# First attention on keys and values brought out of the latents, two heads at once on halves of the array, with the search, the decays and the second block's latents reordered

## What is computed

```python
# dsa_attention: cq (256 wide) and ckv (128 wide) are normed latents
q = jnp.einsum('btr,rhd->bthd', cq, w_uq)                        # 8 heads of 64
q_abs = jnp.einsum('bthd,hcd->bthc', q, w_uk) * (HD_ATT ** -0.5)
_, sel = lax.top_k(score, topk)                                  # 256 of the causal keys
logits = (jnp.einsum('bthc,btkc->bthk', qa, kv_sel) + bias)      # bias: by head and distance
p = jax.nn.softmax(logits, axis=-1)
o = jnp.einsum('bthk,btkc->bthc', p, kv_sel)
return jnp.einsum('bthc,hcd->bthd', o, w_uv)
# second block: q_lat and kv_lat are 384 and 256 wide, k_rope 32
q = (_rmsnorm(q_lat, g_q_lat[i]) @ w_q_up[i]).reshape(bsz, s, N_HEADS, QK_DIM)
kv = (_rmsnorm(kv_lat, g_kv_lat[i]) @ w_kv_up[i]).reshape(bsz, s, N_HEADS, NOPE_DIM + V_DIM)
```

## Time and profile before

| | us |
|---|---|
| median of 3 runs (3828.99 to 3829.85) | 3829.42 |
| the profiled execution | 3827.32 |
| its span | 3826.0 |
| PE, DVE, ACT, POOL busy | 3473.7, 1779.5, 917.6, 345.7 |

### The profile page before, as it was taken

One profiled execution on the slowest core, in us unless ns is written; L12 is line 12 of the kernel. 1 busy time (PEld: TensorE's weight loads), 2 busy tenths in 40 slices (PEclk: granted clock), 3 DMA queues, 4 the chain that ended last, 5 costly groups with the idle time before them and its releaser, 6 DMA issues.

```text
span 3826.0 us, 51800 instructions
## 1 busy us (share of the span) xinstructions
PE 3473.7 (91%) x21830; PEld 2725.6 (71%) x21846; DVE 1779.5 (47%) x2886; ACT 917.6 (24%) x1666; POOL 345.7 (9%) x277
## 2 busy tenths in 40 slices
PE   6989658887889899999997898999999999999998
...
GB/s 202 43 67 209 127 18 52 36 41 12 17 56 61 116 55 48 47 50 83 94 132 57 34 1 23 50 28 50 37 90 132 55 50 45 50 45 115 143 105 149
DMA packets 216071, 270.22 MB, mean 71 GB/s; under 512 B 11068, under 2 KB 176226, under 8 KB 215587
## 3 DMA queue, kind: packets, MB, share of 16 engines
...
...
## 4 chain that ended last, share of the span: by engine, by line
PE 75%; DVE 8%; ACT 3%; issue 2%; POOL 0%; DMA 0%; DVEq 0%; ACTq 0%; POOLq 0%
PE psum L1934 17%; PE psum L1936 17%; PE psum L1938 17%; PE psum L2951 3%; PE psum L1174 3%; PE psum L1706 2%; PE psum L1729 2%; PE psum L2800 2%; PE psum L2448 2%; PE psum L2654 2%; PE psum L2822 2%; PE psum L2811 1%; PE psum L1717 1%; PE psum L1192 1%; PE psum L1760 0%
## 5 line engine op out<-in xcount | busy, mean ns | idle before, releaser
L1934 PE MATMUL psum<-hT_hi,wcut_lo 128*128 128x512 f32 x1856 | 588.9, 394 | 16.8 <-DVE hT_lo L1973 16.8
L1938 PE MATMUL psum<-hT_lo,wcut_hi 128*128 128x512 f32 x1856 | 582.0, 390 | 0.0
L1936 PE MATMUL psum<-hT_hi,wcut_hi 128*128 128x512 f32 x1856 | 581.9, 390 | 0.0
L1934 PEld LDWEIGHTS psum<-hT_hi,wcut_lo 128*128 128x128 f32 x1856 | 350.0, 189 | 96.7 <-DVE hT_lo L1973 17.9
L1938 PEld LDWEIGHTS psum<-hT_lo,wcut_hi 128*128 128x128 f32 x1856 | 349.8, 188 | 73.4
L1936 PEld LDWEIGHTS psum<-hT_hi,wcut_hi 128*128 128x128 f32 x1856 | 350.1, 189 | 72.7
L1916 DVE CAST wcut_hi<-raw 128x1024 fp32r<-128x1024 f32 x256 | 176.9, 691 | 475.0 <-PE psum L1938 450.5
L1934 PE MATMUL psum<-wcut_hi,xcut_lo 128*128 128x512 f32 x1120 | 348.1, 392 | 19.0 <-DVE xcut_lo L2052 13.8
L1936 PE MATMUL psum<-wcut_hi,xcut_hi 128*128 128x512 f32 x1120 | 346.7, 391 | 0.0
L1938 PE MATMUL psum<-wcut_lo,xcut_hi 128*128 128x512 f32 x1120 | 346.5, 391 | 0.0
L1033 POOL TENSOR_TENSOR st<-st,nhalf 128x1 f32<-128x1 f32 (+2 forms) x78 | 62.0, 802 | 3046.3 <-DVE st L674 3046.3
...
## 6 DMA issues: line engine op xcount, KB each, us to landing
...
```

The costliest lines, as they stand in the source:

```text
L1934: pe.matmul(outs[i], al, bs[i][0], start=start, stop=False, skip_group_check=True)
L1936: pe.matmul(outs[i], ah, bs[i][0], start=False, stop=False, skip_group_check=True)
L1938: mm = pe.matmul(outs[i], ah, bs[i][1], start=False, stop=stop, skip_group_check=True)
```

## The change

It has three parts. Lines of the changed kernel differ from those of before by up to 45.

**RWKV.** The search gets 2 steps a round up to round 20 and then 1, after the round's own work; `Pe` goes ahead of `mx`, `PC` ahead of the square of `kk`; PE no longer waits for the fence `rwkv_start`.

```diff
+    K.wuk, K.wuv = r.take("wuk", 8, 64), r.take("wuv", 8, 64)
+    r, mid, last = region(HI0 + 4224, W1), region(2 * SLOT, 4 * SLOT), region(4 * SLOT, 5 * SLOT)
+    K.qT1 = [r.take("qTa", 1024) for _ in range(2)]
+    K.kT1 = [r.take("kTa", 1024)]
...
-    K.ya = r.take("ya", 8, 512)
+    K.Va, K.kT1 = r.take("Va", 8, 512), K.kT1 + [r.take("kTa", 1024)]
...
+    K.Mh += [mid.take("Mh", 1024) for _ in range(2)]
+    K.Lg += [last.take("Lg", 1024), e.take("Lg", 1024)] + [mid.take("Lg", 1024) for _ in range(2)]
...
+
+
+def best_steps(g):
+
+    return 2 if g < 21 else 1
...
     if j == 2:
+        v.wait_ge(*S.at(("Pi", t)))
+        v.scalar_tensor_tensor(Pe, sig, 0.5 * E05, bank(K, 7), MUL, ADD).then_inc(*V.up(("Pe", t)))
         v.wait_ge(*G.at(("mixed", t)))
         v.tensor_tensor(mx, mx, K.prev[:, 0:1024], ADD).then_inc(*V.up(("mx", t)))
-        v.wait_ge(*S.at(("Pi", t)))
-        v.scalar_tensor_tensor(Pe, sig, 0.5 * E05, bank(K, 7), MUL, ADD).then_inc(*V.up(("Pe", t)))
...
         s.wait_ge(*V.at(("Pe", t)))
         s.activation(K.Pes[t % 3], K.Pes[t % 3], ACT.Exp, bias=K.mask("shift")[:, 2:3]).then_inc(*S.up(("Pe", t)))
+        s.wait_ge(*T.at(("tot", t)))
+        s.activation(K.PCs[:, t % 4, :], p[:, 0:8], ACT.Exp, bias=K.mask("shift")[:, 3:4]).then_inc(*S.up(("PC", t)))
         if t:
             s.wait_ge(*V.at(("bonus", t - 1)))
         s.wait_ge(*V.at(("kk", t)))
         s.activation(K.tmp, K.kk, ACT.Square).then_inc(*S.up(("kk", t)))
-        s.wait_ge(*T.at(("tot", t)))
-        s.activation(K.PCs[:, t % 4, :], p[:, 0:8], ACT.Exp, bias=K.mask("shift")[:, 3:4]).then_inc(*S.up(("PC", t)))
...
 def rwkv_tensor(pe, K):
-    rwkv_start(pe, K)
     pe.wait_ge(*K.D["mk"].at("mk"))
...
     for g, tiles in rounds_of():
-        if g < BEST_ROUNDS:
-            for _ in range(3):
-                next(K.best, None)
-        if g == BEST_ROUNDS:
-            for _ in K.best:
-                pass
         for t, r in tiles:
...
                 front_vector(v, K, t, r)
+        if g < BEST_ROUNDS:
+            for _ in range(best_steps(g)):
+                next(K.best, None)
+        if g == BEST_ROUNDS:
+            for _ in K.best:
+                pass
```

```diff
-ATT = [(h, t) for h in range(8) for t in range(NT)]
+ORDER = (4, 3, 5, 2, 6, 1, 7, 0)
+ATT = [(q, t) for q in range(4) for t in ORDER]
...
-        sp.wait_ge(*V.at(("max", h - 2, NT - 1)))
+        if h >= 4:
+            sp.wait_ge(*V.at(("max", 8 * (h // 2) - 9, h % 2)))
         distances_load(sp, K, h)
-    sp.wait_ge(*T.at(("qa", 7)))
-    loads_to(sp, K, "w_out", 3, "w_out")
+        if h == 5:
+            sp.wait_ge(*T.at(("query", 3, 1)))
+            loads_to(sp, K, "w_out", 3, "w_out")
+    fence(sp, K, "att")
...
+def query_tensor(pe, K, q, j, b):
+
...
+    pe.wait_ge(*B.free(b))
+    if j < 2:
+        for k in range(2):
+            mm = pe.matmul(bank(K, b), w[:, k, q * 128:(q + 1) * 128], K.cqT2[:, k, hs], start=k == 0, stop=k == 1, skip_group_check=True)
+    else:
+        mm = pe.matmul(bank(K, b), K.wuk[:, 2 * q:2 * q + 2, :].rearrange("p a b -> p (a b)"), K.ckvT2[:, hs], start=True, stop=True,
+                       skip_group_check=True)
+    mm.then_inc(*T.up(("query", q, j)))
+    B.until(b, S if j < 2 else V, ("query", q, j))
...
+def values_tensor(pe, K, t, b):
...
+    pe.wait_ge(*B.free(b))
+    pe.matmul(bank(K, b), K.ckvT2[:, t * 128:(t + 1) * 128], K.wuv.rearrange("p a b -> p (a b)"), start=True, stop=True,
+              skip_group_check=True).then_inc(*T.up(("values", t)))
+    B.until(b, S if t % 2 else V, ("values", t))
...
+def scores_tensor(pe, K, r):
...
+    for b in range(4):
+        pe.wait_ge(*B.free(b))
+    for o in range(0, W, 512):
+        n = min(512, W - o)
+        for par in range(2):
+            d = slice(64 * par, 64 * par + 64)
+            mm = pe.matmul(bank(K, 2 * par, 2)[:, o:o + n], K.qT1[q % 2][d, t * 128:(t + 1) * 128], K.kT1[q % 2][d, o:o + n], start=True,
+                           stop=t < 2, skip_group_check=True)
+            if t < 2:
+                mm.then_inc(*T.up(("qk", r, par)))
...
+        pe.wait_ge(*V.at("maskb"))
+        for par in range(2):
+            for o in range(0, W, 512):
+                n = min(512, W - o)
+                mm = pe.matmul(bank(K, 2 * par, 2)[:, o:o + n], K.idbf, K.maskb[:, MOFF[t] + o:MOFF[t] + o + n], start=False, stop=True,
...
+            mm.then_inc(*T.up(("qk", r, par)))
+    for par in range(2):
+        for b in (2 * par, 2 * par + 1):
+            B.until(b, V, ("max", r, par))
...
+def turned_tensor(pe, K, r, par):
...
+    L = K.Lg[2 * (r % 3) + par]
+    pe.wait_ge(*V.at(("norm", r, par)))
...
+        for k in range(g0, min(t + 1, g0 + 4)):
+            tr = pe.transpose(bank(K, b)[:, (k - g0) * 128:(k - g0 + 1) * 128], L[:, k * 128:(k + 1) * 128], K.ident)
...
+def outputs_tensor(pe, K, r):
...
+    pe.wait_ge(*B.free(6))
+    for par in range(2):
+        pe.wait_ge(*S.at(("pT", r, par)))
+    for b in range(t + 1):
+        for par in range(2):
+            mm = pe.matmul(bank(K, 6)[64 * par:64 * par + 64, 0:128], K.Va[:, b, (2 * q + par) * 64:(2 * q + par + 1) * 64],
+                           K.pT[2 * (r % 2) + par][:, b, :], start=b == 0, stop=b == t, skip_group_check=True)
+    mm.then_inc(*T.up(("pv", r)))
+    B.until(6, V, ("mixed in", r))
...
+    for j in range(4):
+        query_tensor(pe, K, 0, j, 7 - j)
+    for t in range(NT):
+        values_tensor(pe, K, t, t if t < 4 else 11 - t)
+    for r in range(len(ATT) + 3):
+            turned_tensor(pe, K, r - 2, 0)
         if r < len(ATT):
+            scores_tensor(pe, K, r)
+        if 2 <= r < len(ATT) + 2:
+            turned_tensor(pe, K, r - 2, 1)
+        if r >= 3:
...
+            outputs_tensor(pe, K, r - 3)
+        if 2 <= r % 8 < 6 and r < 24:
+            query_tensor(pe, K, r // 8 + 1, r % 8 - 2, 7)
...
+    v.tensor_tensor_reduce(out=K.Lg[i][:, 0:W], in0=bank(K, 2 * par, 2)[:, 0:W], in1=K.Mh[h % 4][:, 896 - 128 * t:896 - 128 * t + W],
+                           scale=1.0, scalar=-3e38, op0=ADD, op1=MAX, accum_out=K.s1[:, 0, i:i + 1]).then_inc(*V.up(("max", r, par)))
...
+    v.tensor_scalar(K.s1[:, 1, i:i + 1], K.s1[:, 0, i:i + 1], -1.0, None, MUL).then_inc(*V.up(("negmax", r, par)))
...
+def normed_vector(v, K, r):
...
+    v.wait_ge(*S.at(("exp", r, 1)))
+    v.reciprocal(K.s1[:, 3, i:i + 2], K.s1[:, 2, i:i + 2]).then_inc(*V.up())
+    v.wait_ge(*V.own())
+    for par in range(2):
+        L = K.Lg[i + par][:, 0:W]
+        v.tensor_scalar(L, L, K.s1[:, 3, i + par:i + par + 1], None, MUL).then_inc(*V.up(("norm", r, par)))
...
     for r in range(len(ATT) + 4):
...
+            q, t = ATT[r - 4]
+            v.wait_ge(*T.at(("pv", r - 4)))
+            v.tensor_copy(K.mixT[:, q, t * 128:(t + 1) * 128], bank(K, 6)[:, 0:128]).then_inc(*V.up(("mixed in", r - 4)))
         if r < len(ATT):
+            for par in range(2):
+                largest_vector(v, K, r, par)
+        if 1 <= r < len(ATT) + 1:
+            normed_vector(v, K, r - 1)
+        if 2 <= r % 8 < 6 and r < 24:
+            query_vector(v, K, r // 8 + 1, r % 8 - 2, 7)
...
     for r in range(len(ATT) + 2):
+        for par in range(2):
+            if r >= 2:
+                turned_scalar(s, K, r - 2, par)
+            if r < len(ATT):
+                weights_scalar(s, K, r, par)
+        if 2 <= r % 8 < 6 and r < 24:
+            query_scalar(s, K, r // 8 + 1, r % 8 - 2, 7)
```

```diff
+def tail_vector(v, K, P, outs=False):

     for n in range(4, NT + 3):
         if n < NT:
             post_mean(v, K, P, n)
+            if outs:
+                post_out_vector(v, K, P, n - 4)
...
+def tail_scalar(s, K, P, outs=False):
     for n in range(4, NT + 4):
         if n < NT:
             post_square(s, K, P, n)
+            if outs:
+                post_out_scalar(s, K, P, n - 4)
...
-    if t % 4 == 0:
+    if t == 0:
         pe.wait_ge(*D["w0" if key == "q" else "w1"].at(("lat2", key)))
-        for E in (V, S):
-            pe.wait_ge(*E.at(("hT", "p2", t + 3)))
+    for E in (V, S):
+        pe.wait_ge(*E.at(("hT", "p2", t)))
...
         v.wait_ge(*S.at(("lat2", "q", 4 * h + 3)))
-    lat2_norm(v, K, ("q",), slice(0, 8), 0, 384, "q normed")
     v.wait_ge(*T.at("pos"))
     v.tensor_copy(K.pos, bank(K, 0)[:, 0:8]).then_inc(*V.up("pos"))
+    lat2_norm(v, K, ("q",), slice(0, 8), 0, 384, "q normed")
...
     lat2_rows_vector(v, K, "k", HALVES[1])
-    v.wait_ge(*S.at(("lat2", "k", 7)))
-    lat2_norm(v, K, ("k", 1), HALVES[1], 384, 256, ("k normed", 1))
     for t in range(0, NT, 2):
         v.wait_ge(*T.at(("qlT", t)))
         for j in range(3):
             v.tensor_scalar(K.qlT[:, j, t * 128:(t + 1) * 128], bank(K, t)[:, j * 128:(j + 1) * 128], col(K, "q_lat", j), None,
                             MUL).then_inc(*V.up(("qlT", t)))
+    v.wait_ge(*S.at(("lat2", "k", 7)))
+    lat2_norm(v, K, ("k", 1), HALVES[1], 384, 256, ("k normed", 1))
...
-    for t in range(4):
```

(3 more changed lines are left out.)

245 lines of the change are left out of this document (81 added, 164 removed).

## The result

The changed kernel takes 3708.07 us (median of 4 runs, 3703.19 to 3718.07), beside 3829.2 of the kernel before: a ratio of 0.9686, 95% interval 0.9668 to 0.9705. That is 121 us less, where 132 were forecast; 3708 lies in the range of 3655 to 3760. The profiled execution took 3703.19, its span is 3701.8, 124.2 less than before.

| stretch, us | before | after | difference | forecast |
|---|---|---|---|---|
| up to the first product of the attention | 890.1 | 892.8 | +2.7 | -31 |
| the attention, up to the first product of `w_out` | 297.1 | 192.7 | -104.4 | -76 |
| `w_out`, FFN, `down` and latents, up to L2699 (before L2654) | 959.8 | 936.2 | -23.6 | -25 |
| the rest | 1679.0 | 1680.2 | +1.2 | 0 |

What follows compares the result with a forecast made beforehand. PE, busy for 91% of the span, was taken as the bound. Attention -76, RWKV -31 and latents -25 make -132 from 3827.3, so 3695, or 3697 us as median; range 3655 to 3760.

Steps and rivals of the forecast that it cites:

- Attention, PE's own work: Attention: PE's scores, masks, turns, products, queries, keys, values and changes of shape sum to 166 us at full clock.
- The rival that column halves do not overlap: Attention: the products with `Va` cost 68 us, 45 more in the stage, total 3742; chance 0.14.
- the factor 1.31: Attention: multiplier on PE's sum for gaps, start, end and half clock, taking 166 to 217 us, a term of -76.
- The cover of the score banks and DVE: Attention: DVE, about 115 us, is not the bound; waits for its maxima are mostly hidden beside turns and products.
- The rival of DVE's loop: Attention: each round's chain of scores, maxima, scaling and turn decides, 247 us, 30 more, total 3727; chance 0.16.
- (a) the search: RWKV: fewer search steps in early rounds save 20 us on DVE, wide tiles' later steps cost 9 (bounds 0 and 19).
- (b) `PC`: RWKV: PE's wait to write bank 7 shrinks in four tiles, 13 us off and 5 more from clock; bounds 3 and 23.
- (c): RWKV: `Pe` ahead of `mx` gains nothing.
- (d): RWKV: the first tile starts without three steps and a fence ahead of it, 2 us off.
- The rival "search and `PC` are swallowed": RWKV: the chain through PE, DVE and POOL stays as it is, +25 us, total 3722; chance 0.08.
- Latents: Second block's latents: `pos` 12.4 and half clock 3, `qlT` 4.6, waits for single tiles and tail the rest; sum -25 us.

Runs made afterwards that it cites:

- together: Changed kernel with both heads' turns ahead of the scores in each attention round; 3757.8 us, ratio 0.9820.
- rising: Changed kernel with query tiles in rising order 0 to 7 within each pair of heads; 3705.5 us, ratio 0.9684.
- quiet: Changed kernel with POOL's three products rk, rkk and brow in RWKV's front moved behind DVE's rrow; 3699.5 us, ratio 0.9672.
- quiet_pc: Kernel of quiet with ACT's order undone, the square of `kk` again ahead of `PC`; 3708.3 us, ratio 0.9692.

## Why the prediction was right, and where it was not

**Attention, PE's own work: right in its parts, and 4% high.** 166 us were forecast at full clock, and at full clock it is 159; that the measured 165.8 looks the same is chance, since it holds 6.7 us of half clock. The scores of two heads overlap, and the products with `Va` cost half (39.2 with the change of shape behind them; 34 and some 5). Turns and products go at 0.109 us where I had 0.118, and the changes of shape come to some 21 us where I had 26. The rival that column halves do not overlap is out. 32 instructions of L1766, each with its own weights, go at 0.055 us apart (1.97 less its tail, by 32). The rule of the Trainium skill, "TensorEngine Tiling (Array Packing)", Restrictions, that column tiling takes away fast weight load, shows no price here; these products are fp32, and no run has another type. The draining at a change of mode, which the Trainium skill states on the same page under Key Properties, agrees with the trace: 1.06 where 0.86 is the work.

**Attention, the factor 1.31: wrong, and this is the term that was mis-sized.** I carried over from the kernel before the ratio of the stage to PE's full-clock sum, 293.7 to 224. Without PE's last wait, for the first weights of `w_out`, the stretch is 188.9 us now, a ratio of 1.14. 217 less 188.9 is the whole 28 us by which the term missed: by the full-clock work of 159, a ratio of 1.19, some 9 of it are the sum and 19 the factor. The factor was not a property of the stage. Of the 40.6 us of waits before, some 22 belonged to the chain that made the latent-space queries (waits of L1760, L1767 and of L1698 for `qa`), which the change removes; and the half level took 27.4 of the 256.5 us of work there, 6.7 now. That the waits brought the lower clock with them no run takes apart from the rest of the change, but run together shows the same link from the other side.

**The cover of the score banks and DVE: right.** DVE was busy for 108 us (I had 115), PE waited 11.3 for the scaling and 3.7 for the maxima. The rival of DVE's loop would have given 30 more. The order of the tiles, to which I had given the credit for this, did nothing (rising); the scores between the turns do it (together).

**RWKV, (a) the search: wrong.** Of the -20, 4 to 10 were there at 580 us (first L1327 at 572.7 to 578.4 against 582.5), and the +9 was mis-sized: the steps of wide tiles cost the whole head start and more by tile 4. A lead of 7.6 us (574.9 for 582.5) is a lag of 6.6 at tile 4's `Pe` (649.2 for 642.6), 14 in all, nearer to the bound of 19 than to 9. The 9 came from DVE's idle share of 40%, and a share doesn't price it: the steps stand in front of what PE waits for, and the clock falls with the waits (0.84 for 0.97 from 575 to 652 us).

**RWKV, (b) `PC`: the wait went as forecast, the time did not.** L1355 waits 1.0 us in place of 4.4. I had taken that as 13 off the end and 5 of clock back; "DVE is late next" stood only as my lower bound of 3, and that is what happened, with 4 us kept in three tiles. Half of the chain was there to be read, before anything ran: DVE took 1.79 us for `Pe` (L1506) and 0.69 for `kk` (L1503), products of the same form. The other half came with the change: L1504 and `kk` slow down only once `PC` is early. quiet and quiet_pc show what both are worth. Neither (c) nor (d) was run by itself, and the 2 us of (d) can't be seen in a scatter of 6. The rival "search and `PC` are swallowed", with a chance of 0.08, is what came true; it deserved far more.

**Latents: right.** -25 forecast, -23.6 measured; `pos` and the clock behind it 15.4 both forecast and measured; the rest 9.6 forecast, 8 measured. `pos` costs its whole price with the rest in place, so the rest doesn't stand in for it; how the 8 are shared out is open.
